# Computing an attention mixer's gate logits with tokens stationary and 48 weight columns moving

## The chip, the cores and the metric

The kernel runs on one core of a Trainium2 chip. The metric is the time on the device of one execution, in microseconds (us), as the median of several runs. TensorE (PE) multiplies: it loads a stationary operand into its array (a weight load, PEld in the profile) and streams a moving operand through it. VectorE (DVE), ScalarE (ACT) and GpSimd (POOL) do the elementwise work, SyncE (SP) issues most DMAs. The engines run on their own and meet at semaphores.

## The reference

Two blocks of two layers each work on 256 tokens of width 1024. The change lies in the last mixer, `_nsa`, an attention with three branches (compressed, selected and window keys), whose outputs are weighted by gates. The gates come from the last 48 columns of the input projection (16 heads times 3 branches):

```python
proj = x @ w_qg                                   # (256, 1024) @ (1024, 1024 + 48)
q = _rmsnorm(proj[..., :N_HEADS * HEAD_DIM].reshape(b, s, N_HEADS, HEAD_DIM), q_norm)
gate = jax.nn.sigmoid(proj[..., N_HEADS * HEAD_DIM:].astype(jnp.float32))
...
out = gc[..., 0:1] * o_cmp + gc[..., 1:2] * o_sel + gc[..., 2:3] * o_win
```

## The kernel before

The program is written engine by engine: each engine has one function for each phase, and the order of its instructions is the order in the source. Nothing is scheduled later, so an engine that waits holds up all that stands behind it.

A float32 product is made of float32r parts. A weight chunk is split into `whi` (ScalarE, line 836) and `wlo` (VectorE, line 1584), the turned activations lie in `x_both` as `xhi` and `xlo`, and three products are summed in PSUM: high by high, high by low, low by high. `KT` is 8, the number of 128-row slices of the 1024 inputs, `TT` is 2, the number of 128-token tiles, `TAIL` is 48, and `P` is 128. Chunks pass through a ring of four `whi`/`wlo` slots.

The last mixer's phase stands in the functions `nsa`. On TensorE it runs as follows. `along` multiplies a token tile by 512 weight columns with the tokens stationary (lines 2536, 2538 and 2547). Two calls of it make the first 512 query columns for both token tiles. Between them stand the compressed keys (line 3078). After the second call come the gates: 24 matmuls, of which 16 are on lines 3084 and 3085 and 8 on line 3087, with the 48 weight columns stationary and all 256 tokens moving. The logits therefore lie turned, 48 partitions by 256 tokens. Then come a transpose of the compressed keys (line 3091), the third call of `along` for the other 512 columns of the first token tile, which has eight transposes of finished queries inside it (`first_turns`, line 3098), two transposes that turn the gates to 128 tokens by 48 (line 3118), the scores against the compressed keys (`cmp_scores`, line 3109), the fourth call of `along`, four transposes of probabilities (line 3129) and the attention itself, with lines 2917, 2921, 3137, 2931, 3167 and 3172.

ScalarE copies query tiles out of PSUM (`keep`, line 1426), applies the sigmoid to the turned logits (line 1458), copies the turned keys (line 1463) and the turned queries (`keep_q`, line 1431), and copies the turned gates (line 1467) ahead of `keep(2)`. VectorE normalises each query tile: lines 1689 to 1691, a root on GpSimd (line 1534), the scaling (line 2346); the softmax of the compressed branch is on lines 2358 to 2381 and uses the gates on line 2375.

The places of the gates in PSUM are in bank 4 both turned and not.

Of the kernel before, what the change touches and what calls it, by code (L numbers as in the profile page):

```python
# [19 lines left out]
ACT = mybir.ActivationFunctionType  # L20
AX = mybir.AxisListType

P = 128
S = 256
TT = S // P
D = 1024
KT = D // P
# [14 lines left out]
TAIL = 48  # L42
# [233 lines left out]
def build(nc, w, out):  # L276

    with ExitStack() as ctx:
# [3 lines left out]
        def sem(name):  # L282
            return ctx.enter_context(nc.semaphore(name))

        chunks = Chunks().plan()
        ps = ctx.enter_context(nc.psum_tensor("ps", [P, 8, 512], F32))
# [7 lines left out]
        xhi, xlo = x_both[:, :, 0, :], x_both[:, :, 1, :]  # L294
# [24 lines left out]
        def area(start, *dims):  # L319
            n = int(np.prod(dims))  # L320
            assert start + n <= 13312
            v = arena[:, start:start + n]
            if len(dims) == 2:
                v = v.rearrange("p (a b) -> p a b", b=dims[1])
            if len(dims) == 3:
                v = v.rearrange("p (a b c) -> p a b c", b=dims[1], c=dims[2])
            return v

        ident = const[:, 0:P]
# [63 lines left out]
        cp = area(2560, TT, NH, 32)  # L393
        cpt = area(3584, NG, S)
        qsq = area(5184, 8, HD)
        gates_t = area(12288, S)[0:TAIL]
        gates = area(12544, TT, TAIL)
        qss = sb("qss", [P, 2, 4, 8])
        qrs = area(12640, 4, 8)
# [113 lines left out]
        q_turned = sem("q_turned")  # L513
        nq_ready = sem("nq_ready")
        gates_ready = sem("gates_ready")
        gates_t_ready = sem("gates_t_ready")
        gates_turned = sem("gates_turned")
        blocks_ready = sem("blocks_ready")
        kc_kept = sem("kc_kept")
        kct_ready = sem("kct_ready")  # L520
# [51 lines left out]
        def by_k(v, k):  # L572
            return v.rearrange("p (k n) -> p k n", k=k)
# [250 lines left out]
        def _(act):  # L824
            at = Place()

            def split(*key, width=2048):

                n = chunks.number[key]
                s = chunks.split_number[n]  # L830
                assert s == at.split
                at.split += 1
                act.wait_ge(landed[chunks.slot(n)], chunks.landed(n))
                if s >= WRING:
                    act.wait_ge(chunk_used, chunks.of_split[s - WRING] + 1)
                act.activation(whi[s % WRING][:, 0:width], raw[chunks.slot(n)][:, 0:width], ACT.Copy).then_inc(split_hi, 1)  # L836
# [22 lines left out]
            def wait_tile(t, name, kind):  # L859

                if t == 0:
                    act.wait_ge(tile_done, BY_TILE.index((name, kind)) + 1)
                else:
                    act.wait_ge(chunk_used, chunks.number[name, kind, 1] + 1)
# [72 lines left out]
            def gelu_sigmoid(a):  # L937
                part = slice(a * 2 * NG * N_CMP, (a + 1) * 2 * NG * N_CMP)
                act.wait_ge(gelu_in, a + 1)
                act.activation(csig[:, part], cz2[:, part], ACT.Sigmoid, scale=2 * float(np.sqrt(2 / np.pi))).then_inc(gelu_sig, 1)  # L940
# [348 lines left out]
            def attention(pairs, branches, pair_out, beside, keep_cmp):  # L1289

                units = pairs * branches
                for i in range(units + 2):
                    if i < units:
                        exps(i, of_banks=True)
                    beside(i)
                    if i >= 2 and (i - 1) % branches == 0:
                        pair = (i - 2) // branches
                        dst, src = pair_out(pair)
                        y_high(pair, i - 1, dst(xhi), src)
                    if 0 <= i - 1 < units:  # L1300
                        keep_probs(i - 1)
                        if i - 1 in CMP_TURNS:
                            keep_cmp(CMP_TURNS.index(i - 1))
                at.att += units
                at.y += pairs
# [115 lines left out]
            def nsa(name):  # L1421

                def keep(n):
                    a, t = n // 2, n % 2
                    wait_tile(t, name, ("first", "q")[a])
                    act.activation(xn[:, t, a * 512:a * 512 + 512], ps[:, n, :], ACT.Copy).then_inc(q_kept, 1)

                def keep_q(n):
                    t, half = n % 2, n // 2
                    act.wait_ge(q_turned, n + 1)  # L1430
                    act.activation(nq[:, 4 * half:4 * half + 4, t * P:(t + 1) * P], by_k(ps[:, 5 + n - n // 2, :], 4), ACT.Copy).then_inc(nq_ready, 1)

                def cmp_exps(hv):
                    act.wait_ge(cmp_shifted, hv + 1)
                    act.activation(cl[:, hv], cl[:, hv], ACT.Exp).then_inc(cmp_exp, 1)

                def beside(i):

                    if i == 1:
                        keep_q(2)  # L1440
                        keep_q(3)
                    if i == 4:
                        cmp_exps(1)
                    if i == NH:
                        split(name, "out", 2)

                def keep_cmp(t):
                    act.wait_ge(cmp_turned, t + 2)
                    act.activation(cpt[:, 2:4, t * P:(t + 1) * P], ps[:, 4:6, 3 * P:4 * P], ACT.Copy).then_inc(cpt_ready, 1)

                split(name, "gates", 0, width=KT * TAIL)
                gelu_sigmoid(1)
                keep(0)
                split(name, "q", 0)
                split(name, "q", 1)
                keep(1)
                act.wait_ge(chunk_used, chunks.number[name, "gates", 0] + 1)
                act.activation(gates_t, ps[0:TAIL, 4, 0:S], ACT.Sigmoid).then_inc(gates_t_ready, 1)
                act.wait_ge(kct_turned, 1)
                act.wait_ge(kct_zeroed, 1)  # L1460
                for side in range(2):
                    half = slice(side * HD, (side + 1) * HD)
                    act.activation(kct[half, :, side, :], by_k(ps[half, 7, 0:NG * N_CMP], NG), ACT.Copy).then_inc(kct_ready, 1)
                keep_q(0)
                keep_q(1)
                act.wait_ge(gates_turned, 1)
                act.activation(gates, ps[:, 4, 0:TT * TAIL].rearrange("p (t n) -> p t n", t=TT), ACT.Copy).then_inc(gates_ready, 1)
                keep(2)
                cmp_exps(0)
                split(name, "out", 0)  # L1470
                split(name, "out", 1)
                keep(3)
                act.wait_ge(cmp_turned, 1)
                act.activation(cpt[:, 0:2, :].rearrange("p g (t s) -> p t g s", t=TT), ps[:, 4, :].rearrange("p (t g s) -> p t g s", t=TT, g=2),
                               ACT.Copy).then_inc(cpt_ready, 1)
                attention(NH // 2, 2, nsa_out, beside, keep_cmp)
                split(name, "out", 3)
                out_product(name)
# [976 lines left out]
        def _(pe):  # L2455
# [15 lines left out]
            def used(mm, *key):  # L2471

                assert chunks.number[key] == at.chunk
                at.chunk += 1
                mm.then_inc(chunk_used, 1)
# [598 lines left out]
            def nsa(name):  # L3074
                along(0, 0, name, "first", between=lambda: turn(name, 1))
                pe.wait_ge(gelu_ready, 1)
                for k in range(2):
                    mm = pe.matmul(ps[0:NG * N_CMP, 2, 0:HD], cz[:, k * NG * N_CMP:(k + 1) * NG * N_CMP], w2sb[:, k, :], start=k == 0, stop=k == 1)
                mm.then_inc(cmp_done, 1)
                along(1, 1, name, "first")  # L3080
                hi, lo = weights(name, "gates", 0, k=KT, width=KT * TAIL)
                gates_out = ps[0:TAIL, 4, 0:S]
                for k in range(KT):
                    pe.matmul(gates_out, hi[:, k, :], xhi[:, k, :], start=k == 0, stop=False)
                    pe.matmul(gates_out, lo[:, k, :], xhi[:, k, :], start=False, stop=False)
                for k in range(KT):
                    mm = pe.matmul(gates_out, hi[:, k, :], xlo[:, k, :], start=False, stop=k == KT - 1)
                used(mm, name, "gates", 0)
                pe.wait_ge(kd_ready, 3)
                c = NG * N_CMP  # L3090
# [22 lines left out]

                pe.wait_ge(kc_kept, 1)
                along(2, 0, name, "q", between=first_turns)
                pe.wait_ge(gates_t_ready, 1)
                for t in range(TT):
                    mm = pe.transpose(ps[:, 4, t * TAIL:(t + 1) * TAIL], gates_t[:, t * P:(t + 1) * P], ident[0:TAIL, 0:TAIL])
                mm.then_inc(gates_turned, 1)
                pe.wait_ge(nq_ready, 2)  # L3120
                pe.wait_ge(kct_ready, 2)
                cmp_scores(0)
# [3 lines left out]
                for t in range(TT):  # L3126
                    for g in range(2):
                        at_c = (2 * t + g) * P
                        mm = pe.transpose(ps[:, 4, at_c:at_c + P], cp[:, t, 4 * g:4 * g + 4, :].rearrange("p h n -> p (h n)"), ident)
# [56 lines left out]
            for half in range(2):  # L3186
                mm = pe.matmul(ps[:, 6 + half, :], ones_row, gain_row[:, half * 512:half * 512 + 512], start=True, stop=True)
# [29 lines left out]
```

## Time and profile before

| what | value |
|---|---|
| time, median of 3 runs | 1608.43 us (1608.4 to 1608.75) |
| time of the profiled execution | 1608.15 us |
| span of its trace | 1606.4 us |
| PE busy | 1593.5 us (99%), 9096 matmuls |
| weight loads busy | 1372.9 us (85%) |
| VectorE, ScalarE, GpSimd busy | 1248.4, 883.8, 71.1 us |
| granted TensorE clock | 1.0 over the span |

The profile is of one execution. A matmul's duration in it includes the time to pass through the array, so matmuls overlap one another; what one costs the engine is the distance from its start to the start of the next. The span's own time lies 1.75 us below the time of the same execution, and that execution 0.28 us below the median.

### The profile page before, as it was taken

How to read it: one execution, taken by the hardware profiler on the slowest of the kernel's cores; microseconds unless marked ns; L12 is line 12 of the kernel's file. 1: busy time of each engine (PE TensorE's matmuls, PEld its weight loads, DVE VectorE, ACT ScalarE, POOL GpSimd, SP SyncE). 2: the span in 40 equal slices, each digit the busy share in tenths (PEclk: the TensorE clock that was granted, in tenths of full speed). 3: DMA queues.
4: the chain of work that ended last, by engine and by line, in shares of the span. 5: the costliest groups of instructions: out<-in, count | busy, mean ns of one | idle time of the engine just before them, and what ended most of it. 6: DMA issues, size and time to landing. Idle time of an engine off the chain costs nothing.

```text
span 1606.4 us, 22387 instructions
## 1 busy us (share of the span) xinstructions
PE 1593.5 (99%) x9096; PEld 1372.9 (85%) x9097; DVE 1248.4 (78%) x1305; ACT 883.8 (55%) x1068; POOL 71.1 (4%) x83
## 2 busy tenths in 40 slices
PE   9999999999999999999999999999999999999999
PEld 7998888879888887888888888888888887788887
DVE  6687799965569997799887688986665577868996
ACT  6455655645555565565544556555443455855563
POOL 0233000000000000000000000000100002000000
PEclk9999999999999999999999999999999999999999
DMA  8435846474484736764464867347545662076641
GB/s 293 158 120 192 275 135 223 138 236 156 149 299 133 236 105 198 247 218 160 146 223 158 266 218 231 110 152 233 192 157 191 209 199 88 9 240 219 231 141 53
DMA packets 231735, 294.81 MB, mean 184 GB/s; under 512 B 7644, under 2 KB 185264, under 8 KB 231634
## 3 DMA queue, kind: packets, MB, share of 16 engines
q1 hardware_dynamic: 226026, 284.33, 53.2%
q10 hardware_dynamic: 5608, 9.06, 2.2%
q8 instruction: 72, 1.18, 0.3%
q14 instruction: 29, 0.24, 0.0%
HBM read 290.75 MB, written 1.57 MB: 182 GB/s over the span
## 4 chain that ended last, share of the span: by engine, by line
PE 90%; DVE 6%; DMA 2%; issue 1%; ACT 1%; POOL 0%; SPq 0%; DVEq 0%; POOLq 0%; ACTq 0%
PE ps L2508 27%; PE ps L2512 14%; PE ps L2714 11%; PE ps L2677 7%; PE ps L2547 3%; PE ps L2536 3%; PE ps L2538 3%; PE ps L2499 2%; PE ps L2496 2%; PE ps L2497 2%; PE ps L2604 2%; PE ps L2606 2%; PE ps L2605 2%; DVE wlo L1584 2%; PE ps L2595 1%; PE ps L2839 1%
## 5 line engine op out<-in xcount | busy, mean ns | idle before, releaser
L1584 DVE TENSOR_TENSOR wlo<-raw,whi 128x2048 fp32r<-128x2048 f32 (+1 forms) x234 | 510.7, 2189 | 150.7 <-ACT whi L836 149.4
L2508 PE MATMUL ps<-x_both,whi 128*128 128x512 f32 x2080 | 496.8, 390 | 0.1
L836 ACT ACTIVATE whi<-raw 128x2048 fp32r<-128x2048 f32 x223 | 422.2, 1905 | 117.1 <-DMA raw<-in_ffn_w_gate_up 46.5
L2508 PEld LDWEIGHTS ps<-x_both,whi 128*128 128x128 f32 x2080 | 386.0, 188 | 78.6 <-issue 0.9
L2512 PEld LDWEIGHTS ps<-x_both,wlo 128*128 128x128 f32 x2080 | 267.5, 191 | 10.6
L2512 PE MATMUL ps<-x_both,wlo 128*128 128x256 f32 x2080 | 270.7, 283 | 0.0
L1594 DVE TENSOR_TENSOR wlo<-arena,whi 128x2048 fp32r<-128x2048 f32 x70 | 160.0, 2286 | 5.6 <-ACT whi L849 5.6
L849 ACT ACTIVATE whi<-arena 128x2048 fp32r<-128x2048 f32 x70 | 134.5, 1922 | 39.2 <-DVE arena L1816 24.8
L2536 PE MATMUL ps<-whi,x_both 128*128 128x512 f32 x232 | 88.5, 392 | 0.1
L2496 PE MATMUL ps<-x_both,whi 128*128 128x256 f32 x352 | 88.4, 289 | 0.0
L2497 PE MATMUL ps<-x_both,wlo 128*128 128x256 f32 x352 | 86.2, 283 | 0.0
L2538 PE MATMUL ps<-wlo,x_both 128*128 128x512 f32 x212 | 82.6, 390 | 0.0
L965 ACT ACTIVATE silu<-ps 128x512 f32<-128x512 f32 x50 | 29.9, 598 | 91.7 <-PE ps L2512 91.7
L973 ACT ACTIVATE hid<-ps 128x512 f32<-128x512 f32 x45 | 26.8, 595 | 84.0 <-PE ps L2512 84.0
L2496 PEld LDWEIGHTS ps<-x_both,whi 128*128 128x128 f32 x352 | 67.3, 191 | 0.2
L2497 PEld LDWEIGHTS ps<-x_both,wlo 128*128 128x128 f32 x352 | 67.4, 191 | 0.2
L2677 PE MATMUL ps<-whi,x_both 128*128 128x512 f32 x208 | 66.8, 391 | 0.0
L900 ACT ACTIVATE x_both<-ps 128x512 fp32r<-128x512 f32 x44 | 25.0, 599 | 65.0 <-PE ps L2595 61.3
L2547 PE MATMUL ps<-whi,x_both 128*128 128x512 f32 x232 | 60.1, 394 | 0.0
L2714 PE MATMUL ps<-whi,hhi 128*128 128x512 f32 x140 | 55.3, 395 | 1.8 <-issue 1.3
L2714 PE MATMUL ps<-whi,hhi_b 128*128 128x512 f32 x140 | 55.2, 395 | 0.6
L2714 PE MATMUL ps<-wlo,hhi 128*128 128x512 f32 x140 | 54.9, 392 | 0.0
(335 smaller groups left out, 2390.6 us busy)
## 6 DMA issues: line engine op xcount, KB each, us to landing
raw<-in_ffn_w_gate_up SPq DMA_DIRECT2D x80, 1024.0 KB, 6.2
raw<-in_ffn_w SPq DMA_DIRECT2D x46, 1024.0 KB, 5.9
arena<-in_ffn_w_down SPq DMA_DIRECT2D x24, 1024.0 KB, 7.9
raw<-in_ffn_w_down SPq DMA_DIRECT2D x20, 1024.0 KB, 5.0
arena<-in_ffn_w SPq DMA_DIRECT2D x16, 1024.0 KB, 7.2
raw<-in_hgrn_w_in SPq DMA_DIRECT2D x14, 1024.0 KB, 5.6
raw<-in_moba_w_in SPq DMA_DIRECT2D x12, 1024.0 KB, 5.2
raw<-in_conv_w_in SPq DMA_DIRECT2D x10, 1024.0 KB, 5.4
```

Of the source, the lines that this page charges most:

```text
L836: act.activation(whi[s % WRING][:, 0:width], raw[chunks.slot(n)][:, 0:width], ACT.Copy).then_inc(split_hi, 1)
L849: act.activation(by_k(whi[s % WRING][:], 4), product_src[j], ACT.Copy).then_inc(split_hi, 1)
L1584: ins = dve.tensor_tensor(wlo[s % WRING][:, part], raw[chunks.slot(n)][:, part], whi[s % WRING][:, part].bitcast(F32), ALU.subtract)
L1594: dve.tensor_tensor(by_k(wlo[s % WRING][:], 4), product_src[j], by_k(whi[s % WRING][:], 4).bitcast(F32), ALU.subtract)\
L2496: pe.matmul(out, hi[:, k, tile], xhi[:, k, :], start=k == 0, stop=False)
L2497: pe.matmul(out, lo[:, k, tile], xhi[:, k, :], start=False, stop=False)
L2508: pe.matmul(ps[:, bank + n, :], hi[:, k, n * P:(n + 1) * P], x_both[:, k], start=k == 0, stop=k == KT - 1, skip_group_check=True)
L2512: mm = pe.matmul(ps[:, bank + n, S:2 * S], lo[:, k, n * P:(n + 1) * P], xhi[:, k, :], start=False, stop=k == KT - 1, skip_group_check=True)
L2536: pe.matmul(out, xhi[:, k, tile], hi[:, k % 4, :], start=k == 0, stop=False)
L2538: pe.matmul(out, xhi[:, k, tile], lo[:, k % 4, :], start=False, stop=False)
L2677: mm = pe.matmul(out, a[:, k, tile], b[:, k, part], start=first and k == 0 and n == 0, stop=last and k == 1 and n == 2, skip_group_check=True)
L2714: mm = pe.matmul(ps[:, PRODUCT_BANK[j], :], a[:, k, :], w_part[:, k, :], start=starts and k == 0 and m == 0, stop=k == 3 and m == 2, skip_ ...
```

## The change

The gates are computed with the tokens stationary and the 48 weight columns moving. For each of the two token tiles, and each of the eight slices of the inputs, three matmuls write 128 tokens by 48 columns: 48 matmuls instead of 24. The order inside a tile is also new: the product with the low part of the activations follows in each slice, where it came last before. The logits then already lie with tokens on partitions, so the two transposes, the buffer `gates_t` and two semaphores go. ScalarE's sigmoid reads the final place and writes `gates`, and its later copy goes.

```diff
@@ ScalarE, nsa @@
                 act.wait_ge(chunk_used, chunks.number[name, "gates", 0] + 1)
-                act.activation(gates_t, ps[0:TAIL, 4, 0:S], ACT.Sigmoid).then_inc(gates_t_ready, 1)
+                act.activation(gates, ps[:, 4, 0:TT * TAIL].rearrange("p (t n) -> p t n", t=TT), ACT.Sigmoid).then_inc(gates_ready, 1)
...
                 keep_q(0)
                 keep_q(1)
-                act.wait_ge(gates_turned, 1)
-                act.activation(gates, ps[:, 4, 0:TT * TAIL].rearrange("p (t n) -> p t n", t=TT), ACT.Copy).then_inc(gates_ready, 1)
                 keep(2)
@@ TensorE, nsa @@
-                gates_out = ps[0:TAIL, 4, 0:S]
-                for k in range(KT):
-                    pe.matmul(gates_out, hi[:, k, :], xhi[:, k, :], start=k == 0, stop=False)
-                    pe.matmul(gates_out, lo[:, k, :], xhi[:, k, :], start=False, stop=False)
-                for k in range(KT):
-                    mm = pe.matmul(gates_out, hi[:, k, :], xlo[:, k, :], start=False, stop=k == KT - 1)
+                for t in range(TT):
+                    gates_out = ps[:, 4, t * TAIL:(t + 1) * TAIL]
+                    tile = slice(t * P, (t + 1) * P)
+                    for k in range(KT):
+                        pe.matmul(gates_out, xhi[:, k, tile], hi[:, k, :], start=k == 0, stop=False)
+                        pe.matmul(gates_out, xhi[:, k, tile], lo[:, k, :], start=False, stop=False)
+                        mm = pe.matmul(gates_out, xlo[:, k, tile], hi[:, k, :], start=False, stop=k == KT - 1)
                 used(mm, name, "gates", 0)
...
                 along(2, 0, name, "q", between=first_turns)
-                pe.wait_ge(gates_t_ready, 1)
-                for t in range(TT):
-                    mm = pe.transpose(ps[:, 4, t * TAIL:(t + 1) * TAIL], gates_t[:, t * P:(t + 1) * P], ident[0:TAIL, 0:TAIL])
-                mm.then_inc(gates_turned, 1)
                 pe.wait_ge(nq_ready, 2)
```

On TensorE, the end of the gates' matmuls before, up to the key transpose (L3091) and the third call of `along` (L2536); the last two numbers of a row are the output's partitions and columns:

```order
L3084 MATMUL ps<-x_both,whi 48x256
L3085 MATMUL ps<-x_both,wlo 48x256
L3087 MATMUL ps<-x_both,whi 48x256 x8
L3091 MATMUL ps<-const,arena 128x60
L2536 MATMUL ps<-whi,x_both 128x512
```

The same place of the change, whose line numbers are 3 to 5 lower:

```order
L3081 MATMUL ps<-whi,x_both 128x48
L3082 MATMUL ps<-wlo,x_both 128x48
L3083 MATMUL ps<-whi,x_both 128x48
L3087 MATMUL ps<-const,arena 128x60
L2531 MATMUL ps<-whi,x_both 128x512
```

What was 8 pairs and a row of 8 is now 16 triples, each output with 128 partitions and 48 columns; what stands behind is the same.

On TensorE, the end of the third call of `along` before, with the query transposes (L3098) and the gate transposes (L3118) ahead of the compressed scores (L3109):

```order
L2547 MATMUL ps<-whi,x_both 128x512 x3
L3098 MATMUL ps<-const,xn 128x128 x8
L2547 MATMUL ps<-whi,x_both 128x512 x5
L3118 MATMUL ps<-const,arena 128x48 x2
L3109 MATMUL ps<-arena 128x30 x8
L2536 MATMUL ps<-whi,x_both 128x512
```

The same place of the change:

```order
L2542 MATMUL ps<-whi,x_both 128x512 x3
L3094 MATMUL ps<-const,xn 128x128 x8
L2542 MATMUL ps<-whi,x_both 128x512 x5
L3105 MATMUL ps<-arena 128x30 x8
L2531 MATMUL ps<-whi,x_both 128x512
```

The two gate transposes are gone and the compressed scores follow `along` at once.

On ScalarE, from the second query tile's copy to the third's (L1426) before:

```order
L1426 ACTIVATE xn<-ps 128x512
L1458 ACTIVATE arena<-ps 48x256
L1463 ACTIVATE arena<-ps 64x4x15 x2
L1431 ACTIVATE arena<-ps 128x4x128 x2
L1467 ACTIVATE arena<-ps 128x96
L1426 ACTIVATE xn<-ps 128x512
```

And of the change:

```order
L1423 ACTIVATE xn<-ps 128x512
L1455 ACTIVATE arena<-ps 128x96
L1460 ACTIVATE arena<-ps 64x4x15 x2
L1428 ACTIVATE arena<-ps 128x4x128 x2
L1423 ACTIVATE xn<-ps 128x512
```

The sigmoid reads 128 by 96 where it read 48 by 256, and no copy stands ahead of the third query tile's.

## Rows read from the trace of the kernel before

**Rows 1.** The page: busy us by engine, then the chain that ended last.
```profile
PE 1593.5 (99%) x9096; PEld 1372.9 (85%) x9097; DVE 1248.4 (78%) x1305; ACT 883.8 (55%) x1068; POOL 71.1 (4%) x83
...
PE 90%; DVE 6%; DMA 2%; issue 1%; ACT 1%; POOL 0%; SPq 0%; DVEq 0%; POOLq 0%; ACTq 0%
```
**Rows 2.** The chain of waits, 1310 to 1356 us: start, length, what.
```profile
1327.84 2.29 DVE wlo L1584
...
1334.16 0.70 DVE xn L2346
...
1337.26 0.50 ACT xn L1426
...
1337.78 0.70 DVE arena L1689
...
1352.17 0.34 DVE arena L2391
...
1352.60 0.84 PE ps L2931 x6
```
**Rows 3.** PE's waits from 1352.6 us to the end: us, times, longest.
```profile
PE ps L2931 <- DVE arena L2391: 0.7, 1, 0.7
```
**Rows 4.** Timeline of PE, the gates and their neighbours: start, busy, engine, line, operation.
```profile
1326.53 0.28 PE L3084 MATMUL ps<-x_both,whi 128*48 128x256 f32 x1
...
1328.41 1.10 PE L3087 MATMUL ps<-x_both,whi 128*48 128x256 f32 x8
1329.43 0.27 PE L3091 MATMUL ps<-const,arena 60*128 60x60 f32 x1
```
**Rows 5.** Timelines of PE: 128 stationary columns, with 256, 60 and 64 moving.
```profile
1214.81 1.12 PE L2512 MATMUL ps<-x_both,wlo 128*128 128x256 f32 x8
1215.78 3.68 PE L2649 MATMUL ps<-arena,raw 128*128 128x60 f32 x32
...
1347.88 2.00 PE L3137 MATMUL ps<-w2sb,junk 128*128 128x64 f32 x16
```
**Rows 6.** Weight loads by shape (stationary rows*columns): busy, mean ns | idle before.
```profile
L2536 PEld LDWEIGHTS ps<-whi,x_both 128*128 128x128 f32 x232 | 43.6, 188 | 9.5 <-issue 0.3
...
L2649 PEld LDWEIGHTS ps<-arena,raw 128*128 128x128 f32 x128 | 14.6, 192 | 0.0
...
L2917 PEld LDWEIGHTS ps<-mask_b,ident_b 128*128 128x128 bf16 x32 | 2.6, 97 | 1.6 <-issue 1.0 <-ACT arena L1275 0.2
...
L3084 PEld LDWEIGHTS ps<-x_both,whi 128*48 128x48 f32 x8 | 1.0, 121 | 0.0
```
**Rows 7.** Timeline of PE, third query tile and what follows; first, another turn.
```profile
1318.49 1.03 PE L2595 MATMUL ps<-const,xn 128*128 128x128 f32 x8
1319.28 1.39 PE L2547 MATMUL ps<-whi,x_both 128*128 128x512 f32 x5
1320.60 0.43 PE L3078 MATMUL ps<-w2sb,arena 128*60 128x64 f32 x4
...
1333.39 0.85 PE L2547 MATMUL ps<-whi,x_both 128*128 128x512 f32 x3
1334.08 0.60 PE L3098 MATMUL ps<-const,xn 128*128 128x128 f32 x4
1334.91 0.66 PE L3098 MATMUL ps<-const,xn 128*128 128x128 f32 x4 [0.23 <-DVE xn L2346]
1335.32 1.40 PE L2547 MATMUL ps<-whi,x_both 128*128 128x512 f32 x5
...
1336.90 1.97 PE L3109 MATMUL ps<-arena 128*128 128x30 f32 x16
```
**Rows 8.** Timeline of ACT: turned queries, gates' copy, third query tile.
```profile
1335.60 0.60 ACT L1431 ACTIVATE arena<-ps 128x512 f32<-128x512 f32 x1 [0.29 <-PE ps L3098]
1337.01 0.25 ACT L1467 ACTIVATE arena<-ps 128x96 f32<-128x96 f32 x1 [0.80 <-PE ps L3118]
1337.15 0.59 ACT L1426 ACTIVATE xn<-ps 128x512 f32<-128x512 f32 x1
```

More of the change, by code:

```diff
@@ L395, in build @@
         qsq = area(5184, 8, HD)
-        gates_t = area(12288, S)[0:TAIL]
         gates = area(12544, TT, TAIL)
@@ L515, in build @@
         gates_ready = sem("gates_ready")
-        gates_t_ready = sem("gates_t_ready")
-        gates_turned = sem("gates_turned")
         blocks_ready = sem("blocks_ready")
```

## The prediction

> **What bounds the kernel now.** I read the page first. PE is busy for 1593.5 us, 99% of the span, and the chain that ended last lies on PE for 90% of the span [rows 1]. Anything that adds to PE's own work will therefore be felt, unless it falls where PE waits. So I went to the chain of waits around the gates. The chain does not run through PE there all the time: from 1327.84 us on it runs through the split of a query chunk on DVE and the scaling of the second query tile on DVE, which ends at 1334.86 [rows 2]. PE meets it at the second half of the query transposes, L3098, with 0.23 us of idle time [rows 7]. From there the chain goes through the last five L2547, the two gate transposes L3118 and ScalarE's gate copy L1467 [rows 7, 8] to its copy of the third query tile L1426, and on through DVE from 1337.78 until L2391 ends at 1352.51, which releases L2931 on PE at 1352.60 [rows 2]. After that PE has no wait of its own until the end; the only one listed from 1352.6 on is that same 0.7 us [rows 3]. So whatever shift reaches L2931 reaches the end of the program at full size. The question is only how large it is.
>
> **The gates' matmuls, before.** The first starts at 1326.53, L3087's eight start at 1328.41 and last 1.10 us with about 0.28 us for one, so they lie (1.10 - 0.28)/7 = 0.117 us apart, and the last of the 24 starts at 1328.41 + 7 x 0.117 = 1329.23 [rows 4]. From the first start to the last are 23 steps, 2.70 us. The next instruction, L3091, starts 0.20 us later, and I leave that step as it is.
>
> **The gates' matmuls, after.** There are 48, so 47 steps. A float32r matmul with fewer than 256 moving columns does not occur in this trace, so the step is bounded by neighbours. The nearest row is L2649: 128 stationary rows and columns, 60 moving columns, sums over eight slices, 32 in a row. By its busy time one step is (3.68 - 0.275)/31 = 0.110 us [rows 5]. It is plain float32, issued as two passes, so each row is one pass. L3137 with 64 moving columns gives (2.00 - 0.275)/15 = 0.115, and L3109 with only 30 moving columns (1.97 - 0.274)/15 = 0.113 [rows 5, 7]. Thus 30, 60 or 64 columns cost the same, which says that the moving side does not set the step; the load of 128 stationary columns does. The float32r load of L2536 takes 188 ns, L2649's 192, while the 48-column load of L3084 takes 121 [rows 6]. These durations contain a fixed part; the difference of 67 to 71 ns over 80 columns is some 0.85 ns a column, or an estimated 0.109 us for 128. I take 0.1095, the nearest row's and this estimate's middle. The upper end among the rows with this load is L2512 with 256 moving columns, (1.12 - 0.283)/7 = 0.120 [rows 5]. So the burst takes 47 x 0.1095 = 5.15 us, and the change in the place where L3091 starts is 5.15 - 2.70 = **+2.45 us**. The order inside a slice costs nothing: `xlo` was already read by the `along` just before.
>
> No load is saved because two matmuls in a row use the same stationary slice: `along` has that pattern already, in L2536 and L2538, and the whole trace has 9097 loads for 9096 matmuls [rows 1].
>
> **What waits on that.** ScalarE waits for the gates and holds two key copies (L1463) behind them. By my estimate they are done near 1332.7 (L3091 at 1329.43 + 2.45 and three short operations), and their first reader, L3109, stood at 1336.90 [rows 4, 7]. The final gates, too, are now there before they were (1337.26), so the softmax waits for neither. The query chunk of the third `along` was split by 1327.84 + 2.29 = 1330.13 [rows 2]; `along` starts one more 0.20 behind L3091, now at 1329.43 + 0.20 + 2.45 = 1332.08, so no new wait. DVE's scaling of the second query tile depends on none of this.
>
> **The idle time that is absorbed.** PE reaches the query transposes at 1334.08 + 2.45 = 1336.53, when DVE has been done since 1334.86. Before, the eight took from 1334.08 to 1335.32, 1.24 us; without the wait the same kind of turn takes 1319.28 - 1318.49 = 0.79 us [rows 7]. **-0.45 us**, so the last five L2547 start +2.00 late.
>
> **The transposes that go.** The last five L2547 before start at 1335.32 and are busy for 1.40 us, so the last ends at 1336.72 and starts 0.39 earlier, at 1336.33; L3109 starts at 1336.90. Without L3118 this distance of 0.57 us becomes one step of (0.85 - 0.39)/2 = 0.23 [rows 7]: -0.34 us on PE. On ScalarE the third tile's copy could start 0.03 us after the last L2547's end, at 1336.75, but it stands behind the gate copy L1467 and starts at 1337.15 [rows 8]: **-0.40 us**. The two copies of the turned queries (L1431, 0.60 us for one [rows 8]) would end near 1338.3, and L3109 wants them at 1336.33 + 2.00 + 0.23 = 1338.56. This cover is thin, 0.25 us; if it is gone, PE loses as much as is missing, which its 0.65 us of waiting at L2931 takes up.
>
> **The sum.** PE at L3109: 2.45 - 0.45 - 0.34 = +1.66. DVE from L1689 on: 2.45 - 0.45 - 0.40 = +1.60. DVE sets L2931, so the end moves by +1.60. Against the profiled execution that is 1608.15 + 1.60 = 1609.75 us; the median of the runs lies 0.28 above, 1608.43 + 1.60 = **1610.0 us**, 0.1% slower. A measurement of this kernel can tell some 0.2%, or 3.2 us, from no change, so this counts as the same.
>
> [...] What the rows show is that a pass of 30 to 64 moving columns costs as much as the load of 128 stationary ones [rows 5, 7]. [...]
>
> **Rival 1: the loads turn out quick.** If a float32r load of 128 columns were cheap when nothing wide covers it, the step could fall to that of L3078, 60 stationary columns: (0.43 - 0.22)/3 = 0.070 [rows 7]. Then 47 x 0.070 = 3.29, and 3.29 - 2.70 - 0.45 - 0.40 = -0.26: 1608.2 us. Against it is the row of L2536, 188 ns, like the 192 of plain float32, which showed its full price; a bf16 load of 128 columns takes 97 [rows 6]. Chance 0.08.
> The Trainium skill, TensorE: Matmul & The Clock Gate, section on fast weight load, says that it is on for 128 weights of any type but FP32. Read so, float32r has it and this rival would hold; the 188 against 97 ns say that it has not.
>
> **Rival 2: all of it is hidden.** The chain before 1334.86 is not PE's [rows 2], so one may think that PE's extra work is free and only the gain of 0.40 us stays: 1608.0 us. It would need 2.45 us of slack at L3098, and there are 0.45. Chance 0.04.
>
> **Rival 3: narrow float32r matmuls are slow.** The type was shown only at 256 and 512 moving columns. If a narrow one took as long as one of 512 columns, 0.23, the burst would take 10.81 us and the end move by 10.81 - 2.70 - 0.45 - 0.40 = +7.3: 1615.7 us. It decides from a step of (3.2 + 3.55)/47 = 0.144 us, where the time goes over 0.2%. For it speaks only that no row excludes it; against it, that plain float32 passes do not show it. Chance 0.07.
>
> **How the numbers follow.** Forecast, with steps of 0.109 to 0.120 and each of the two savings present or absent, 1610.0 (0.109 and both) to 1611.4 (0.120 and neither, 5.64 - 2.70 = +2.9), and a few tenths either side: 0.79. The three rivals take 0.19, and 0.02 is left for a shift in DMA or code loading that no row shows, half to each side. The range goes from rival 1's 1608.2 to 1611.4, which holds over 0.8. Faster by over 0.2% is half of what is left, 0.01; slower, rival 3 and the rest, 0.08; within, 0.91.
>
> **What would show it.** The 48 matmuls' starts should lie 0.109 to 0.120 us apart, with loads of 188 to 192 ns. The 0.23 us before L3098 should be gone, the third tile's copy should follow the last L2547 within 0.05 us, DVE's L1689 should start 1.6 us later than 1337.78 and L2931 1.6 us later than 1352.60, with the same distance from there to the end. The forecast is wrong if the step is outside that span, or if a wait appears in front of L2536 or L3109 that is not there now.

## The result and the profile after

The changed kernel takes 1612.94 us (median of 8 runs, 1610.81 to 1616.48), the kernel before beside it 1608.38 us (8 runs, 1608.12 to 1608.75). The ratio is 1.0029 with a 95% interval of 1.002 to 1.0038: slower by 0.29%, or 4.6 us, beyond the range that was forecast (1608.2 to 1611.4), and with nine times the spread (5.7 us for 0.6). The profiled execution took 1614.07 us.

The page shows more work on PE and a granted clock that is no longer full in one of the 40 slices:

```profile
span 1612.3 us, 22430 instructions
...
PE 1600.2 (99%) x9118; PEld 1379.1 (86%) x9119; DVE 1248.2 (77%) x1305; ACT 882.5 (55%) x1067; POOL 70.6 (4%) x83
...
PEclk9999999999999999999999999999999998999999
...
PE 94%; DVE 4%; DMA 1%; ACT 0%; issue 0%; POOL 0%; DVEq 0%; POOLq 0%; ACTq 0%; SPq 0%
```

A slice is 40 us wide and its digit hides most of it (9 is 90% or more). The busy times by stretch of the same trace (us, then busy us of PE, PEld, DVE, ACT and POOL with counts, granted clock, DMA share, GB/s) put the place and the depth beside each other:

```profile
1326.00:1330.00 4.00, 4.00 (x38) 3.96 (x37) 3.56 (x3) 1.84 (x2) 2.44 (x1) 1.00 0.44 116
1330.00:1336.00 6.00, 6.00 (x23) 5.11 (x23) 3.34 (x6) 0.68 (x3) 1.65 (x1) 0.55 0.73 274
1336.00:1340.00 4.00, 4.00 (x21) 3.29 (x19) 0.00 (x0) 0.17 (x1) 0.00 (x0) 0.82 0.00 0
1360.00:1365.00 5.00, 5.00 (x38) 3.85 (x39) 3.47 (x12) 0.80 (x3) 0.00 (x0) 0.66 0.02 3
```

The kernel before has 1.00 in all these stretches. Here the clock stands at half, the level of 1.2 GHz, for 6.8 us that begin inside the gates' burst, and again for 3.4 us in the attention (the share that is missing in each stretch, counted as time at half clock). PE is listed as busy for the whole of it. Its timeline tells the cost of one instruction at either level:

```profile
1326.08 0.18 PE L3081 MATMUL ps<-whi,x_both 128*128 128x48 f32 x1
1326.11 0.27 PE L3082 MATMUL ps<-wlo,x_both 128*128 128x48 f32 x1
1326.22 0.27 PE L3083 MATMUL ps<-whi,x_both 128*128 128x48 f32 x1
...
1330.35 0.27 PE L3081 MATMUL ps<-whi,x_both 128*128 128x48 f32 x1
1330.47 0.29 PE L3082 MATMUL ps<-wlo,x_both 128*128 128x48 f32 x1
1330.58 0.39 PE L3083 MATMUL ps<-whi,x_both 128*128 128x48 f32 x1
1330.79 0.39 PE L3081 MATMUL ps<-whi,x_both 128*128 128x48 f32 x1
...
1332.18 0.36 PE L3087 MATMUL ps<-const,arena 60*128 60x60 f32 x1
1332.47 0.79 PE L2531 MATMUL ps<-whi,x_both 128*128 128x512 f32 x1
...
1336.47 0.63 PE L2533 MATMUL ps<-wlo,x_both 128*128 128x512 f32 x1
1336.90 0.63 PE L2531 MATMUL ps<-whi,x_both 128*128 128x512 f32 x1
...
1339.99 1.40 PE L2542 MATMUL ps<-whi,x_both 128*128 128x512 f32 x5
1341.23 1.86 PE L3105 MATMUL ps<-arena 128*128 128x30 f32 x16
```

The narrow matmuls start 0.112 us apart until 1330.58, then 0.21; the wide ones of `along` behind them start 0.43 us apart where they had 0.23 [rows 7]. L3087 is the key transpose, L2531, L2533 and L2542 are the L2536, L2538 and L2547 of before. The third query tile's copy and the first instruction of VectorE that waits for it are:

```profile
1341.43 0.60 ACT L1423 ACTIVATE xn<-ps 128x512 f32<-128x512 f32 x1 [0.51 <-PE ps L2542]
1342.06 0.69 DVE L1684 TENSOR_TENSOR arena<-xn 128x512 f32<-128x512 f32 x1 [7.67 <-ACT xn L1423]
```

A chain piece answers to the last of [rows 2]:

```profile
1356.88 0.85 PE ps L2926 x6
```

### The profile page after: what moved, and what is told of

The parts are those of the page before. It is cut to its first block, busy times and chain, and to the rows that moved or that the text cites. A ratio compares the mean times of both kernels' runs of the same rounds, so it can differ in the third digit from the quotient of the medians.

```text
span 1612.3 us, 22430 instructions
## 1 busy us (share of the span) xinstructions
PE 1600.2 (99%) x9118; PEld 1379.1 (86%) x9119; DVE 1248.2 (77%) x1305; ACT 882.5 (55%) x1067; POOL 70.6 (4%) x83
## 4 chain that ended last, share of the span: by engine, by line
PE 94%; DVE 4%; DMA 1%; ACT 0%; issue 0%; POOL 0%; DVEq 0%; POOLq 0%; ACTq 0%; SPq 0%
PE ps L2503 29%; PE ps L2507 15%; PE ps L2709 12%; PE ps L2672 7%; PE ps L2531 3%; PE ps L2542 3%; PE ps L2533 3%; PE ps L2494 2%; PE ps L2491 2%; PE ps L2492 2%; PE ps L2599 2%; PE ps L2600 2%; PE ps L2601 2%; PE ps L2590 1%; PE ps L2916 1%; DVE wlo L1579 1%
## 5 line engine op out<-in xcount | busy, mean ns | idle before, releaser
L2531 PE MATMUL ps<-whi,x_both 128*128 128x512 f32 x232 | 90.0, 398 | 0.1
L2533 PE MATMUL ps<-wlo,x_both 128*128 128x512 f32 x212 | 83.9, 396 | 0.0
L2542 PE MATMUL ps<-whi,x_both 128*128 128x512 f32 x232 | 60.1, 394 | 0.0
```

Source lines behind the costliest of these rows:

```text
L2531: pe.matmul(out, xhi[:, k, tile], hi[:, k % 4, :], start=k == 0, stop=False)
L2533: pe.matmul(out, xhi[:, k, tile], lo[:, k % 4, :], start=False, stop=False)
```

## Where the time went

I measure from the first gate matmul, 1326.53 before [rows 4] and 1326.08 after. DVE's L1684 starts 15.98 us behind it, where L1689 started 11.25 behind [rows 2]: +4.73. L2926 starts 30.80 us behind it, where L2931 started 26.07: +4.73. From there to the end of the span are 255.42 us against 253.80: +1.62. Together that is 6.35 us; less the 0.45 us by which this execution came sooner to the gates it is 5.9 us, the difference of the spans (1612.3 and 1606.4). So there are two losses with a fall of the clock in each, +4.73, of which I had forecast 1.60, and +1.62, of which I had forecast nothing.

My theory after the result, A: the row of 48 matmuls that stream 48 columns each makes the granted clock fall, and the excess over 1609.9 us is that. Rivals: B, the narrow form has a cost of its own (by number of matmuls and loads, or by its place) and the fall is chance or a consequence; C, narrow matmuls let the clock fall wherever they stand, however they are spread.

## The experiments

All are timed beside the kernel before on the same chip, in three sets of three or four kernels. "The clock of a run" below is its mean over the whole span, rounded to three places; it says whether the clock fell in a run, but only a trace says where. Before had medians of 1608.27, 1608.21 and 1608.3 us in them (32, 33 and 24 runs).

**More columns at the same step (w128, w256).** Only the moving operand is widened. The 80 or 208 added columns of the output are read by nobody.

```diff
-                    gates_out = ps[:, 4, t * TAIL:(t + 1) * TAIL]
+                    gates_out = ps[:, 4, t * 128:(t + 1) * 128]
...
-                        pe.matmul(gates_out, xhi[:, k, tile], hi[:, k, :], start=k == 0, stop=False)
...
+                        part = slice(k * TAIL, k * TAIL + 128)
+                        pe.matmul(gates_out, xhi[:, k, tile], whi[n_gates][:, part], start=k == 0, stop=False)
...
```

Expected of the first:

> The changed kernel, but each of the 48 gate matmuls streams 128 columns instead of 48 (the 48 wanted ones and 80 that nobody reads), so the number of matmuls, their loads and their order stay. Theory A, the clock: the long row of matmuls that stream only 48 columns lets the granted clock fall to half, and this is what lies above the predicted 1610.0. Then more columns at the same step (the load of 128 columns sets it, 0.112 us in the changed kernel's trace) keep the clock up: 1610 to 1610.5 us, clock 1.00 everywhere, spread of the runs under 0.6 us. Rival B, the loss is in the number of matmuls and loads or in the order of the work, and the clock fell by chance: 1612 to 1614 with the same spread as the change.

And of the second:

> The same with 256 streamed columns, 208 of which nobody reads. The step rises to 0.120 us, as for 256 columns in the kernel before, so 47 x 0.008 = 0.4 us more than at 0.112. Theory A: clock 1.00, 1610.4 to 1611 us, small spread. Rival B: 1612.4 to 1614.5 us.

Measured: w128 1610.46 us (11 runs, 1609.98 to 1611.63), ratio 1.0015 (1.0006 to 1.0023); w256 1611.83 us (11 runs, 1609.88 to 1612.49), ratio 1.0018 (1.0009 to 1.0027). The clock by stretch in w128:

```profile
1326.00:1330.00 4.00, 4.00 (x34) 3.85 (x33) 3.55 (x2) 2.40 (x2) 3.07 (x1) 1.00 0.29 66
1330.00:1336.00 6.00, 6.00 (x37) 5.24 (x37) 3.97 (x7) 0.64 (x3) 1.64 (x1) 1.00 0.84 311
1336.00:1340.00 4.00, 4.00 (x30) 3.57 (x28) 0.36 (x1) 2.06 (x4) 0.00 (x0) 1.00 0.00 0
1360.00:1365.00 5.00, 5.00 (x40) 3.45 (x36) 2.33 (x10) 2.78 (x11) 0.00 (x0) 0.75 0.00 0
```

The fall at the gates is gone with the number, the loads and the order of the matmuls unchanged, and B goes with it. The runs agree: 8 of 11 with 128 columns and 5 of 11 with 256 have a clock of 1.000, where the change has none in its first eight nor in the eight repeated below. What I had not expected is the last row: the later fall, in the attention, still comes. A mean clock below 1.000 have 3 of 11 runs of w128 and 6 of 11 of w256 (the trace of w256, too, has its one fall in the attention), which is why their medians lie apart; the runs with 1.000 have medians of 1610.29 and 1610.45 us. The two widths do not tell each other apart. This trace also allows to check the forecast's sum without a fall at the gates. Its first gate matmul starts at 1326.71, and these lines follow:

```profile
1339.64 0.69 DVE L1684 TENSOR_TENSOR arena<-xn 128x512 f32<-128x512 f32 x1 [4.62 <-ACT xn L1423]
...
1354.45 0.85 PE L2926 MATMUL ps<-const,arena 128*128 128x128 f32 x6 [0.65 <-DVE arena L2386]
```

12.93 and 27.74 us behind the first gate matmul, against 11.25 and 26.07: +1.68 and +1.67 us, where the forecast had +1.60 for both.

**Two bursts (split) and half the work (one_tile).** In the first the second token tile's 24 matmuls stand behind the compressed scores; in the second they are left out.

```diff
-                for t in range(TT):
+                for t in range(1):
```

That is one_tile, in which ScalarE reads the first tile's logits for both. In split, `gates_tile(0)`, the loop's body for the first tile, stands where both tiles stood, and ScalarE's sigmoid stands behind its copy of the third query tile:

```diff
                 cmp_scores(0)
+                used(gates_tile(1), name, "gates", 0)
```

> The changed kernel with its 48 matmuls in two bursts of 24: the second token tile's stand behind the compressed scores, ScalarE's sigmoid behind its copy of the third query tile. The same work, each burst 2.7 us. Theory A, if what counts is an unbroken row of narrow matmuls: no fall at the first burst; behind the scores, which are narrow too (30 columns), there may be one. Without a fall 1610 to 1611 us, with one 1612 or more. Rival B: 1612 to 1614 us with clock 1.00 or not.

Measured: 1611.74 us (10 runs, 1610.97 to 1613.87), ratio 1.0023 (1.0014 to 1.0032), the clock below 1.000 in all ten runs. The trace shows where:

```profile
1336.82 1.86 PE L3108 MATMUL ps<-arena 128*128 128x30 f32 x16
1338.52 0.27 PE L3082 MATMUL ps<-whi,x_both 128*128 128x48 f32 x1
```

```profile
1326.00:1330.00 4.00, 4.00 (x31) 3.73 (x30) 3.56 (x2) 2.60 (x3) 3.17 (x1) 1.00 0.29 72
1336.00:1341.00 5.00, 5.00 (x44) 4.83 (x42) 2.73 (x7) 1.06 (x2) 1.60 (x1) 1.00 0.00 0
1341.00:1345.00 4.00, 4.00 (x14) 3.25 (x14) 2.15 (x7) 3.56 (x4) 0.04 (x1) 0.57 0.02 4
```

The first burst of 24 has no fall behind it. The second stands directly behind the sixteen passes of 30 columns, makes a row of 40 narrow ones with them, and the clock falls at its end, at 1341. So the row may be made of several lines: the sixteen scores alone have no fall behind them in before or in w128, with the 24 gate matmuls behind them they have.

> The changed kernel with the first token tile's 24 gate matmuls alone; the second tile's gates are not computed and take the first one's. Theory A: no fall of the clock, and the rest of my sum can be read without it: 2.7 us less burst than the change's 5.3, so 24 steps of 0.112 instead of before's 24 of 0.117, no transposes: -0.1 - 0.40 us and no wait absorbed, 1607.9 to 1608.3 us. Rival B, a fixed cost of about 3 us that the narrow form brings whatever its number: 1610 to 1611 us.

Measured: 1608.16 us (11 runs, 1607.42 to 1610.18), ratio 0.9999 (0.999 to 1.0008), no fall at the gates in the trace, as expected:

```profile
1326.00:1330.00 4.00, 4.00 (x31) 3.74 (x30) 3.55 (x2) 2.94 (x5) 2.95 (x1) 1.00 0.31 77
1330.00:1336.00 6.00, 5.55 (x29) 4.48 (x28) 3.84 (x7) 1.00 (x3) 1.64 (x1) 1.00 0.80 302
```

**The same 48 narrow matmuls between wide ones (mixed, mixed2).** Nothing is left out or widened.

```diff
+                    for half in range(2):
+                        pe.matmul(ps[:, 2, :], xhi[:, k, 0:P], parts[k // 4][half][:, k % 4, :], start=k == 0 and half == 0, stop=False)
+                        next(two)
+                        next(two)
...
```

This is mixed2, in the third call of `along`; each `next(two)` issues one gate matmul. Here ScalarE's sigmoid too stands behind its copy of the third query tile. mixed did it in the second call.

> The changed kernel's 48 narrow gate matmuls, none left out, but put between the 512-column matmuls of the query tile's second call of along: two behind each of twelve, then three behind each of eight. Same instructions, same loads, no long row of narrow ones. Theory A, the long row lets the clock fall: clock 1.00 around the gates, 1610.0 to 1610.5 us where the later fall (in the attention) does not come, 1611.5 where it comes. Rival, the fall comes from the number of narrow matmuls wherever they stand: 1611.8 us or more with the clock at 0.5 within ten us of the gates.

Measured: 1611.53 us (11 runs, 1610.99 to 1613.21), ratio 1.0019 (1.001 to 1.0028). The clock is 1.000 in ten of eleven runs and 1.00 in each stretch of the trace around the gates, but the time is a microsecond above what I expected of A. The trace has another cause for that:

```profile
1336.96 0.60 PE L3122 MATMUL ps<-const,xn 128*128 128x128 f32 x4
1338.97 0.66 PE L3122 MATMUL ps<-const,xn 128*128 128x128 f32 x4 [1.42 <-DVE xn L2341]
```

The second query tile was finished later, since gate matmuls now stood inside its `along`, and the wait of 0.23 us at the query transposes [rows 7] grew to 1.42. I had overlooked that the gates' place behind the second tile was what hid them from VectorE's chain. Hence mixed2:

> The 48 narrow gate matmuls again between wide ones, now two behind each of the 24 matmuls of the third call of along, so that the second query tile is not held back as in mixed; the sigmoid stands behind the third tile's copy. Theory A, the fall needs an unbroken row of narrow matmuls: clock 1.00 there and 1610.4 us (the change's 1609.9 without a fall, and some 0.5 us in which PE waits for the query chunk's split, since it comes to it 2.7 us sooner). Rival, the fall comes from the number of narrow matmuls: 1612.5 us and more.

Measured: 1610.86 us (11 runs, 1610.23 to 1612.7), ratio 1.0016 (1.0008 to 1.0025); the clock is 1.000 in nine of eleven runs, and their median is 1610.86. One wait, at the place expected, for the split of the query chunk:

```profile
1327.85 0.47 PE L3124 MATMUL ps<-whi,x_both 128*128 128x512 f32 x1 [0.64 <-DVE wlo L1579]
1328.15 0.18 PE L3110 MATMUL ps<-whi,x_both 128*128 128x48 f32 x1
1328.18 0.27 PE L3112 MATMUL ps<-wlo,x_both 128*128 128x48 f32 x1
1328.29 0.48 PE L3124 MATMUL ps<-wlo,x_both 128*128 128x512 f32 x1
```

```profile
1330.00:1336.00 6.00, 6.00 (x42) 5.46 (x41) 4.10 (x7) 0.00 (x0) 1.64 (x1) 1.00 0.85 322
```

All 48 are there and the clock stays. That ends C. The time is 0.46 us above the expected 1610.4. The expectation's base of 1609.9 was too low: the undisturbed runs of w128 have 1610.29, and with the wait of 0.64 us that makes 1610.93. One question stays open: mixed2 and w128 both stream more columns in the same stretch than the change does, so no run here tells an unbroken row of narrow matmuls from a stretch in which few columns stream.

**A burst of 36 (burst36).** The second tile's sum runs over half of the inputs only.

```diff
-                    for k in range(KT):
+                    for k in range(KT - 4 * t):
...
```

> The changed kernel with a burst of 36 instead of 48 narrow matmuls: the second token tile's gates are summed over half of the inputs only. Without a fall: 12 x 0.112 = 1.3 us less than 1609.9, so 1608.6 us. Theory A, with the fall's chance growing with the length of the row: 24 had none in the profile, 48 always; here some of the runs at 1608.6 and some 1.5 to 3 us above. If the fall needs nothing but narrow matmuls: all of them above 1610.

Measured: 1611.28 us (11 runs, 1607.75 to 1613.08), ratio 1.0015 (1.0006 to 1.0024). Ten of eleven runs have a clock below 1.000, at 1609.49 to 1613.08 us, and the eleventh 1.000 at 1607.75. So with one and the same program the clock falls in one run and not in another. The trace has two falls:

```profile
1327.00:1331.00 4.00, 4.00 (x38) 3.97 (x36) 3.56 (x4) 1.62 (x3) 2.21 (x1) 1.00 0.52 145
1331.00:1336.00 5.00, 5.00 (x16) 3.90 (x17) 3.10 (x6) 0.61 (x3) 1.65 (x1) 0.66 0.82 305
```

The first begins near 1331.9, some 1.2 us behind the start of the last narrow matmul (1330.67) and with wide ones already running. The second is the one in the attention (0.74 from 1360 to 1365). The clock of a run does not tell the two apart, so ten of eleven is not the share of runs that fell behind the burst. The single undisturbed run is 0.85 us below the 1608.6 expected; one run does not settle that.

**The load by itself (halves).** The kernel before, each of its 24 matmuls cut in two of 128 tokens.

```diff
-                    pe.matmul(gates_out, hi[:, k, :], xhi[:, k, :], start=k == 0, stop=False)
...
+                        pe.matmul(gates_out[:, tile], hi[:, k, :], xhi[:, k, tile], start=k == 0, stop=False)
...
```

> The kernel before with each of its 24 gate matmuls (48 stationary columns) cut in two of 128 moving tokens, so 48 matmuls as in the change, but with loads of 48 columns. It prices the load: if the load of the stationary columns sets the step, it is now near 0.07 us as for 60 stationary columns, and the time 47 x 0.070 - 2.70 - 0.45 = +0.1 us: 1608.4 us. If a fixed cost for each float32r matmul or load set the 0.112 us, the step stays there and the time is +2.1 us: 1610.4. No fall of the clock expected by theory A, since 128 columns stream in each.

Measured: 1608.62 us (11 runs, 1607.91 to 1610.08), ratio 1.0002 (0.9993 to 1.0011).

```profile
1327.31 0.64 PE L3089 MATMUL ps<-x_both,whi 128*48 128x128 f32 x8
```

The step is (0.64 - 0.22)/7 = 0.060 us, even below the 0.070 expected. Forty-eight matmuls with 48 stationary columns cost what 24 with twice the tokens cost (2.88 and 2.81 us); with the same 128 moving columns and 128 stationary ones the step is 0.112 (w128). So the count is free and the stationary load is what the change pays for.

**A delay without narrow matmuls (shift).** Eight unread matmuls of 512 columns in front of the gates of the kernel before.

```diff
+                spare = whi[chunks.split_number[chunks.number[name, "gates", 0]] % WRING]
+                for k in range(8):
+                    pe.matmul(ps[:, 4, :], xhi[:, k, 0:P], spare[:, 0:512], start=True, stop=True)
```

> The kernel before with eight added matmuls of 512 columns in front of the gates, whose result nobody reads: a delay of 8 x 0.226 = 1.8 us of dense work, and no narrow matmul more. 0.45 us of it are absorbed at the query transposes: 1609.7 us. This asks whether the second fall, 5 us behind the scores in the attention, comes more often because that place lies later. If a delay alone brings it: a good part of the runs at 1611 us and above, as in w128 and w256. If not: all within 1609.4 to 1610.1 us.

Measured: 1610.05 us (11 runs, 1608.97 to 1612.05), ratio 1.0011 (1.0002 to 1.002). Seven runs have a clock of 1.000 and a median of 1609.82 us, the sum's 1609.7 (1.81 us of work less the 0.45 absorbed). In four the clock is below 1.000. Before had 2 of 32, 5 of 33 and 5 of 24 such runs. So the clock falls in the kernel before as well, more seldom. Where it falls there is not shown: the traces of before and of shift have no fall. Four of eleven against twelve of 89 is too little to say that a delay alone makes it more frequent.

**The second saving alone (late_turn).** The kernel before with the gate transposes behind the scores and the gates' copy behind `keep(2)`.

```diff
-                act.wait_ge(gates_turned, 1)
-                act.activation(gates, ps[:, 4, 0:TT * TAIL].rearrange("p (t n) -> p t n", t=TT), ACT.Copy).then_inc(gates_ready, 1)
                 keep(2)
+                act.wait_ge(gates_turned, 1)
+                act.activation(gates, ps[:, 4, 0:TT * TAIL].rearrange("p (t n) -> p t n", t=TT), ACT.Copy).then_inc(gates_ready, 1)
...
```

> The kernel before with its two gate transposes behind the compressed scores and ScalarE's copy of the gates behind the copy of the third query tile; nothing is left out, the gates keep 48 stationary columns. It takes the change's second saving alone. By my sum VectorE's chain starts 0.40 us sooner and the transposes cost PE 0.34 us that its wait of 0.65 us at L2931 covers: 1607.9 us against 1608.3. If the saving was not real (the copy of the third tile bound by something else): 1608.3 to 1608.7 us.

Measured: 1607.91 us (11 runs, 1607.15 to 1609.68), against 1608.3; the ratio is 0.9997 (0.9988 to 1.0006), so it is no proven gain, but it is the value forecast, and the trace shows the mechanism: the third tile's copy waits for PE's L2547 alone, and the transposes follow the scores.

```profile
1336.40 0.60 ACT L1426 ACTIVATE xn<-ps 128x512 f32<-128x512 f32 x1 [0.56 <-PE ps L2547]
...
1351.84 0.85 PE L2931 MATMUL ps<-const,arena 128*128 128x128 f32 x6 [0.41 <-issue]
```

```profile
1336.20 1.86 PE L3109 MATMUL ps<-arena 128*128 128x30 f32 x16
1337.99 0.32 PE L3121 MATMUL ps<-const,arena 48*128 48x48 f32 x2
```

The first gate matmul of this trace starts at 1326.19 and VectorE's L1689 at 1337.03. That is 10.84 us to L1689 and 25.65 to L2931, against 11.25 and 26.07 in before: the chain came 0.41 and 0.42 us sooner. It is the lowest median of all versions that compute everything.

**The change once more (again).**

> The changed kernel unaltered, on the chip of mixed2 and late_turn. Theory A: every run above 1610.5 us, with a clock of 0.999 or less in each, 1611 to 1616 us, and no two falls of the same length. If the first result was one chip's: some runs at 1610 us with clock 1.00.

Measured: 1612.36 us (8 runs, 1611.17 to 1614.77), ratio 1.0025 (1.0014 to 1.0035). All eight runs have a clock of 0.996 to 0.999, as all eight of the first result had. In this trace the clock falls some 6.1 us behind the first gate matmul, in the first 4.4, so behind the burst instead of inside it: the last narrow matmul, at 1332.45, has its full speed.

```profile
1332.45 0.27 PE L3083 MATMUL ps<-whi,x_both 128*128 128x48 f32 x1
1332.65 0.27 PE L3087 MATMUL ps<-const,arena 60*128 60x60 f32 x1
1332.85 0.50 PE L2531 MATMUL ps<-whi,x_both 128*128 128x512 f32 x1
1333.19 0.55 PE L2533 MATMUL ps<-wlo,x_both 128*128 128x512 f32 x1
1333.53 0.63 PE L2531 MATMUL ps<-whi,x_both 128*128 128x512 f32 x1
...
1341.76 0.69 DVE L1684 TENSOR_TENSOR arena<-xn 128x512 f32<-128x512 f32 x1 [6.16 <-ACT xn L1423]
```

This trace has no fall in the attention, so it prices the one at the gates alone. L1684 starts 14.47 us behind the first gate matmul (1327.29), where w128 had 12.93: +1.54 us for a fall of 3.4 us. L2926, at 1356.58, starts 29.29 us behind it for 27.74: +1.55. From there to the end are 253.8 us, as before. The expectation that no two falls are of the same length did not come true: of the falls in the traces, the gates' fall of the first result lasted 6.8 us and the others (gates in burst36 and again, behind the scores in split, in the attention in the first result, w128, w256 and burst36) 3.4 each.

## Why the prediction was wrong

**What bounds the kernel** was read rightly. A shift at the gates reached L2931 at full size and, apart from the clock, the end.

**The step of the narrow matmuls**, put at 0.1095 us between 0.109 and 0.120, measured 0.112: 47 x 0.112 = 5.26 for 5.15. A load of 128 float32r columns sets it, as halves shows from the other side. Rival 1, quick loads, and rival 3, slow narrow float32r, are both out. The Trainium skill, TensorE: Matmul & The Clock Gate, section on fast weight load, says that it is on for 128 weights of any type but FP32. If float32r counted as such a type the step would have been that of rival 1, 0.070 by its estimate; the measured 0.112 us are against it.

**The idle time and the transposes** came as forecast: no wait of PE is left at the query transposes, the third tile's copy follows the last L2542, and late_turn gives the second saving alone at its 0.4 us in the trace (its median, 0.39 us below before, is within the noise). The sum of +1.60 us up to L2931 is +1.67 in w128, whose clock held there.

**The step that failed** stood nowhere in the sum: that every instruction behind and inside the burst would run at the clock of before. I costed 48 narrow matmuls at rows taken at full clock, and took for granted that the burst would not change the clock. None of the three rivals had this mechanism; the slow one put its 7 us on the narrow matmul's own duration. It costs 4.73 - 1.67 = 3.06 us at the gates in the first trace, and 1.62 us in the attention. These 4.68 us, the 1.67 of the sum, less the 0.45 by which this execution came sooner to the gates, are the 5.9 us between the two spans. The other trace of the same program has one fall of half the length at the gates, +1.54 us, and none in the attention. So falls that differ in number and length from run to run are a cause of the spread, which I had not forecast either; that they are all of it is not shown, since the other runs have no trace.

The rows to see it in were there. L2649's 32 passes of 60 columns keep the clock, and so do the L3109 of [rows 7]; I could have noticed that the change makes a row 1.4 times as long as the longest narrow one that the trace showed (5.3 us against 3.7), with nothing that says what the clock does then. That belonged on the upper side of the range, as a fall whose price no row of before gave.

The Trainium skill, TensorE: Matmul & The Clock Gate, part 1 (the HAM clock gate), says that the chip gates this clock by how busy the array has been and draws from it the rule to avoid idle gaps. The trace goes further than that rule: PE was listed as busy for 4.00 of the 4.00 us ahead of the fall and had no gap; only what each matmul streams was small. The granted clock fell to the lower of the page's two levels and no other.

What is **shown**: that the fall at the gates comes with the row of narrow matmuls (w128 widens them, mixed2 spreads them, one_tile halves the row, and it is gone in the trace of each; split builds a row of two parts, and it is back), and that the excess over the forecast in the first trace is the two falls. What stays **open**: first, whether the row must be unbroken or only few columns may stream in the stretch; second, what brings the later fall, in the attention, which the traces of the change, w128, w256 and burst36 show. Runs whose mean clock is below 1.000 are 3, 6, 4 and 3 of 11 in w128, w256, shift and one_tile, 1 and 2 of 11 in mixed and mixed2, 1 and 3 of 11 in halves and late_turn, and 12 of 89 in before; for most of them no trace tells the place. The attention has narrow matmuls of its own in every version (L3109 and L3167 of before). The counts do not say whether the work in front of it matters.

## What to carry to other kernels

Make the smaller dimension the stationary one when loads bound the step: 48 stationary columns with 256 tokens moving cost 0.117 us for what two matmuls at 0.112 us do the other way round, and the two transposes that this form needs cost 0.3 to 0.4 us, which leave the path if they stand off it (late_turn). Before a long row of narrow matmuls is put on TensorE, look at the granted clock of the narrow stretches that exist and at how long they are; if the new one is longer, put wide matmuls between them, or stream more columns at the same step, and price the case where the clock falls on all that stands behind. Here both remedies kept the clock at the gates and neither made the change pay: w128 took 1610.46 us and mixed2 1610.86, against 1608.3 before. With a program whose runs differ by more than before, look at the clock of each run first: here the spread, not the median, was the first sign.

## What the runs showed of the hardware

- TensorE's granted clock fell from full to half while PE was busy without a gap, in or behind a row of narrow matmuls: in both traces with 48 matmuls of 48 moving columns, in the one with 36, and in split's with 16 of 30 columns and 24 of 48. No trace with 24 alone (one_tile, the first burst of split) shows it at that place. By their mean clock all 16 runs of the change had a fall somewhere, and ten of eleven with 36.
- A fall lasted 3.4 us in seven cases and 6.8 us in one. At the gates one of 3.4 us put the rest back by 1.54 us (again) and the one of 6.8 by 3.06 (first result); in the attention one of 3.4 us cost 1.62 there, and 1.55 in w128 (255.35 us from L2926 to the end for 253.80).
- At half clock a float32r matmul of 512 columns starts every 0.43 us instead of 0.23, a 128-column load with 48 moving columns every 0.21 instead of 0.112.
- With 48 stationary columns and 128 moving ones the step is 0.060 us; with 128 stationary ones it is 0.112 whether 48 or 128 columns move.
- Raising the moving columns from 48 to 128 left the step at 0.112 us and kept the clock at the gates.
